# Feed-forward: the gated rows turned by VectorE in 32x32 blocks into SBUF, in place of fp32 transposes on TensorE through PSUM

## The reference

```python
h2 = _rmsnorm(x, g_ffn[l])
x = x + (jax.nn.silu(h2 @ w_ffn_gate[l]) * (h2 @ w_ffn_up[l])) @ w_ffn_down[l]   # D_FF = 2816
```

## Time and profile before

| | us |
|---|---|
| three runs | 1134.68, 1134.51, 1134.10 |
| median | 1134.51 |
| profiled execution | 1134.34 |
| its span | 1132.5 |
| TensorE busy | 1120.9 (99%) |
| VectorE busy | 710.5 (63%) |
| ScalarE busy | 633.9 (56%) |
| GpSimd busy | 213.2 (19%) |

### The profile page before, as it was taken

The page is one execution under the profiler, slowest core; times in us unless marked ns, Lnnn a source line. Parts: engine busy times, 40 slices in busy tenths (PEclk is TensorE's granted clock), DMA queues, the critical chain, the costliest instruction groups (busy, mean ns, idle before and its releaser), DMA issues.

```text
span 1132.5 us, 14165 instructions
## 1 busy us (share of the span) xinstructions
PE 1120.9 (99%) x5380; PEld 931.6 (82%) x5380; DVE 710.5 (63%) x721; ACT 633.9 (56%) x787; POOL 213.2 (19%) x127
## 2 busy tenths in 40 slices
PE   8999999999999999999999999999999999999998
PEld 7788887888888888888778888888888888888886
DVE  5745758676554543695338568984465776798442
ACT  6655566655767642654478365663355545566431
POOL 1424700000343410000013012420006100333000
PEclk9999999999999999999999999999999999999999
DMA  9644444545555455565434545565555334465630
GB/s 355 232 170 176 153 145 146 207 172 198 183 180 195 173 198 186 212 243 186 149 112 162 191 172 214 191 222 186 187 192 198 117 143 167 154 218 186 223 112 37
DMA packets 30502, 205.14 MB, mean 181 GB/s; under 512 B 3625, under 2 KB 3793, under 8 KB 6769
## 3 DMA queue, kind: packets, MB, share of 16 engines
q1 hardware_dynamic: 28752, 198.75, 48.8%
q0 software_dynamic: 1696, 5.64, 1.6%
HBM read 203.33 MB, written 1.05 MB: 180 GB/s over the span
## 4 chain that ended last, share of the span: by engine, by line
PE 93%; DVE 2%; issue 2%; POOL 1%; DMA 1%; ACT 1%; SPq 0%; DVEq 0%; POOLq 0%
PE ps L689 72%; PE ps L1185 8%; PE ps L1187 4%; PE aux L761 3%; PE ps L811 1%; PE aux L976 1%; PE aux L962 1%; DMA mrows<-in_mem 1%; DMA grow<-in_b_gate 1%; POOL sc L510 0%; PE aux L1123 0%; PE aux L1074 0%; DVE Wl L1867 0%; DVE sc L1939 0%; PE aux L1137 0%
## 5 line engine op out<-in xcount | busy, mean ns | idle before, releaser
L1867 DVE TENSOR_TENSOR Wl<-raw,Wh 128x2048 fp32r<-128x2048 f32 x184 | 451.9, 2462 | 255.4 <-ACT Wh L1318 254.9
L689 PE MATMUL ps<-Wh,xT 128*128 128x512 f32 x1536 | 486.7, 393 | 0.0
L1318 ACT ACTIVATE Wh<-raw 128x2048 fp32r<-128x2048 f32 x184 | 350.0, 1907 | 231.7 <-PE ps L689 228.5
L689 PEld LDWEIGHTS ps<-Wh,xT 128*128 128x128 f32 x1536 | 288.4, 188 | 60.3 <-issue 1.2
L689 PE MATMUL ps<-Wl,xT 128*128 128x512 f32 x768 | 299.0, 389 | 0.0
L689 PEld LDWEIGHTS ps<-Wl,xT 128*128 128x128 f32 x768 | 144.3, 188 | 29.4 <-issue 0.5
L1185 PE MATMUL ps<-xT,Wh 128*128 128x512 f32 x384 | 133.6, 394 | 0.0
L1187 PE MATMUL ps<-xT,Wl 128*128 128x256 f32 x384 | 106.4, 277 | 0.0
L689 PE MATMUL ps<-Wh,hTh 128*128 128x512 f32 x256 | 99.7, 389 | 0.0
L689 PE MATMUL ps<-Wh,hTl 128*128 128x512 f32 x256 | 99.6, 389 | 0.0
L689 PE MATMUL ps<-Wl,hTh 128*128 128x512 f32 x256 | 99.6, 389 | 0.0
(11 more groups left out here) (359 smaller groups left out, 1363.7 us busy)
## 6 DMA issues: line engine op xcount, KB each, us to landing
raw<-in_wstream SPq DMA_DIRECT2D x185, 1024.0 KB, 4.7
grow<-in_post_gains POOLq DMA_DIRECT2D x4, 512.0 KB, 5.8
grow<-in_b_gate POOLq DMA_DIRECT2D x6, 256.0 KB, 3.5
mrows<-in_mem SPq DMA_DIRECT2D x2, 512.0 KB, 5.4
raw<-in_wstream SPq DMA_DIRECT2D x2, 512.0 KB, 6.5
x<-in_x SPq DMA_DIRECT2D x1, 1024.0 KB, 13.4
out<-x SPq DMA_DIRECT2D x4, 256.0 KB, 2.0
rdm<-in_ret_decays POOLq DMA_DIRECT2D x1, 768.0 KB, 5.4
```

The source lines that it names most:

```text
L689: mm = nc.tensor.matmul(ps[2 * pair + t][:, :], a[:, kt, t * P:(t + 1) * P], w[:, slot, j, :], start=(first and j == 0 and q == 0), stop=( ...
L1318: nc.scalar.activation(Wh[:, slot, 0:nk, :], raw[:, slot, 0:nk, :], ACT.Copy).then_inc(hi_ready, 1)
L1867: nc.vector.tensor_tensor(Wl[:, slot, 0:nk, :], raw[:, slot, 0:nk, :], Wh[:, slot, 0:nk, :].bitcast(F32), ALU.subtract).then_inc(lo_ready, 1)
```

## The change

The gated rows don't go through TensorE and PSUM. VectorE turns them: 16 instructions, each of which takes a block of 32 partitions (tokens 32a to 32a+31 of both token tiles) and 32 columns of each of the two k-tiles, 128 elements per partition, turns it in 32x32 blocks and writes it to partitions 32b to 32b+31 of a new SBUF tile `ffT` with two buffers. They follow in `ff` behind the second low part of the granules and wait for `ff_h`. The log-sigmoid moves ahead of the first low part, `ff_low(n-1)` between the two. ScalarE's `ff_high` and VectorE's `ff_low` read `ffT` in place of `aux`; ScalarE's wait ahead of the read-outs is for the turn of unit n-2. TensorE has no transposes in this stage; before each granule of `ffd0` it waits for the low parts by a count.

```diff
--- before.py
+++ after.py
@@ -163,8 +163,6 @@
     use("foT", [0, 1, 2, 3])
     use("mgT", [0, 1, 2, 3])
     use("x1T", [0, 1, 2, 3])
-    for n in range(FFN // 256):
-        use(f"ffT{n}", [n % 2])
     use("x2T", [0, 1, 2, 3])
     use("rqT0", [0, 1])
     use("rqT1", [2, 3])
@@ -354,6 +352,7 @@
         ffTl = at("ffTl", [P, FFK, TOK], R + 22, F32R)
         gu = at("gu", [P, 2, 2, C], R + 44)
         fe = at("fe", [P, 2, 2, 256], R + 52)
+        ffT = at("ffT", [P, 2, 2, TOK], R + 56)
         RQ = at("RQ", [P, 2, D], R)
         RK = at("RK", [P, 2, D], R + 8)
@@ -1050,7 +1049,7 @@
                           (1, 0): half_ready("mgT", 2), (1, 1): half_ready("mgT", 3), (1, 2): next_tile("x1T", x, added("wout1"), 0)})
-            def ff_unit(n, i=None, between=None):
+            def ff_unit(n, i=None):
                 name = f"ffn{n}"
@@ -1060,35 +1059,18 @@
                 for q in range(2):
                     g = G[name] + q
-                    if q and between:
-                        between()
                     granule(g % RING, g + 1 if i is None else i * 4 + (g + 1), xTh, xTl, range(4 * q, 4 * q + 4),
                             U[name] % 2, q == 0, q == 1, read_out)
-            def ff_turned(n, i=None):
-                pe.wait_ge(sem("ff_h"), n + 1 if i is None else i * 2 + (n + 1))
-                k, use = AUX[(f"ffT{n}", 0)]
-                pe.wait_ge(aux_free[k], use - 1 if i is None else i + (use - 1))
-                for kk in range(2):
-                    for t in range(2):
-                        tr = nc.tensor.transpose(aux[k][:, kk * TOK + t * P:kk * TOK + (t + 1) * P],
-                                                 gu[:, n % 2, t, kk * P:(kk + 1) * P], ident)
-                tr.then_inc(aux_ready[k], 1)
             begin(["ffn0", "ffn1"], "x1T", x, added("wout1"))
-            ff_unit(2, None, lambda: ff_turned(0))
-            ff_turned(1)
+            ff_unit(2)
             with pe.Fori(1, 5) as i:
                 for n in (1, 2):
                     ff_unit(n, i)
-                    ff_turned(n - 1, i)
             def ff_ready(q):
                 def go_on():
-                    if q == 3:
-                        ff_turned(10)
-                    for n in range(2 * q, min(2 * q + 2, FFN // 256)):
-                        wait_operand(f"ffT{n}", (0,))
+                    pe.wait_ge(sem("ff_low"), min(2 * q + 2, FFN // 256))
                 return go_on
             product("ffd0", (ffTh, ffTl), before={q: ff_ready(q) for q in range(6)})
@@ -1587,7 +1569,7 @@
                 split(G[name] + RING, i)
                 count = n if i is None else i * 2 + n
                 if n >= 2 or i is not None:
-                    act.wait_ge(sem("ff_h"), count - 1)
+                    act.wait_ge(sem("ff_turned"), count - 1)
                 for t in range(2):
                     if t == 0:
                         act.wait_ge(half_done, count + (U["ffn0"] + 1))
@@ -1608,11 +1590,10 @@
                 nc.scalar.activation(fe[:, n % 2, :, :], fe[:, n % 2, :, :], ACT.Exp).then_inc(sem("ff_rec"), 1)
             def ff_high(n, i=None):
-                k, use = AUX[(f"ffT{n}", 0)]
-                act.wait_ge(aux_ready[k], use if i is None else i + use)
+                count = n if i is None else i * 2 + n
+                act.wait_ge(sem("ff_turned"), count + 1)
                 dst = ffTh[:, :, :].rearrange("p (n k) t -> p n k t", k=2)
-                nc.scalar.activation(dst[:, n if i is None else i * 2 + n, :, :], aux[k][:, :], ACT.Copy)\
-                    .then_inc(sem("ffT_hi"), 1)
+                nc.scalar.activation(dst[:, count, :, :], ffT[:, n % 2, :, :], ACT.Copy).then_inc(sem("ffT_hi"), 1)
             act.wait_ge(sem("norm_rstd"), NORMS["x1"])
             ff(0)
@@ -2196,31 +2177,41 @@
             cross(GEND["wout1"], "x1T", "g_ffn", mixed)
             x_stats("x1")
-            def ff(n, i=None):
+            def ff(n, i=None, low=True):
                 name = f"ffn{n}"
+                log_sigmoid(fe[:, n % 2, :, :], gu[:, n % 2, :, 0:256], n + 2 if i is None else i * 2 + (n + 2))
                 split(G[name] + RING, i)
-                log_sigmoid(fe[:, n % 2, :, :], gu[:, n % 2, :, 0:256], n + 2 if i is None else i * 2 + (n + 2))
+                if low:
+                    ff_low(n - 1, i)
                 split(GEND[name] - 1 + RING, i)
+                ff_turn(n, i)
+            def ff_turn(n, i=None):
+                dve.wait_ge(sem("ff_h"), n + 1 if i is None else i * 2 + (n + 1))
+                for a in range(4):
+                    for b in range(4):
+                        ins = nc.vector.transpose(ffT[32 * b:32 * b + 32, n % 2, :, :].rearrange("p k (t j) -> p k t j", j=P)
+                                                  [:, :, :, 32 * a:32 * a + 32],
+                                                  gu[32 * a:32 * a + 32, n % 2, :, 0:256].rearrange("p t (k j) -> p k t j", j=P)
+                                                  [:, :, :, 32 * b:32 * b + 32])
+                ins.then_inc(sem("ff_turned"), 1)
             def ff_low(n, i=None):
-                k, use = AUX[(f"ffT{n}", 0)]
                 count = n if i is None else i * 2 + n
                 dve.wait_ge(sem("ffT_hi"), count + 1)
                 lo = ffTl[:, :, :].rearrange("p (n k) t -> p n k t", k=2)
                 hi = f32(ffTh).rearrange("p (n k) t -> p n k t", k=2)
-                nc.vector.tensor_tensor(lo[:, count, :, :], per_kt(aux[k], 2), hi[:, count, :, :], ALU.subtract)\
-                    .then_inc(aux_free[k], 1)
-            ff(0)
+                nc.vector.tensor_tensor(lo[:, count, :, :], ffT[:, n % 2, :, :], hi[:, count, :, :], ALU.subtract)\
+                    .then_inc(sem("ff_low"), 1)
+            ff(0, low=False)
             ff(1)
-            ff_low(0)
             ff(2)
-            ff_low(1)
             with dve.Fori(1, 5) as i:
                 for n in (1, 2):
                     ff(n, i)
-                    ff_low(n - 1, i)
             for g in range(G["ffd0"], GEND["ffd0"] - 1):
                 split(g + RING)
                 if g == G["ffd0"] + 2:
```

## The result

| | us |
|---|---|
| before, median of 4 runs | 1134.47 (1134.1 to 1134.68) |
| after, median of 4 runs | 1150.27 (1149.67 to 1151.29) |
| ratio | 1.0142, 95% interval 1.0129 to 1.0154 |
| predicted | 1151 (1133 to 1168) |
| span of the profiled execution, before / after | 1132.5 / 1147.9 |

A forecast was written before the change was run, and what follows sets the result against it. TensorE (99% busy) bounds the kernel before; after the change VectorE sets the pace at 13.0 us a unit against 10.92. From 1134.34 us, -4.8 of transposes and +21.8 of stalls give +17, so 1151 us (1133 to 1168).

The forecast's parts named there:

- The removed term: TensorE's four transposes in each of 11 units, 0.44 us a unit, all on the path: 4.8 us saved.
- The price of a transpose: VectorE, 16 per unit: 0.32 us each from start to start, a turn of 5.1 us (3.4 to 6.6).
- The exclusion: VectorE and GpSimd instructions with two SBUF inputs exclude each other in the loop; 2.3 us of VectorE's period.
- My sequence of who waits for whom: Per unit: log-sigmoid, split to 2.90, first product 4.07, subtraction 4.63, second product 5.8, second split 7.96, transposes to 13.0 us.
- The period: VectorE's time per feed-forward unit: 13.0 us against TensorE's 10.92, so VectorE sets the pace.
- the sum: Whole feed-forward stretch: -4.8 us of transposes and +21.8 of stalls, +17 us, giving 1151 us.
- First stall: TensorE ahead of unit 3: split done at 308.1, TensorE free at 306.4, 1.7 us lost.
- the 21.8 I had as stalls: TensorE waiting for VectorE's splits, some 2 us in each of eleven places, +21.8 us.
- The first: Rival, VectorE: order blocks but transposes overlap at 0.21 us each, period 11.3, 1132 us; chance 0.11.
- The second: Rival: VectorE keeps up, no exclusion that matters, period 10.8, TensorE is the bound, 1129.6 us; chance 0.07.
- The third: Rival, VectorE: a transpose is dearer than the reduction, 0.36 to 0.45 us, 1158 to 1174 us; chance 0.15.
- The fourth: Rival: TensorE's granted clock falls because of the stalls, adding to the rest, over 1174 us; chance 0.04.

The follow-up runs named there:

- the first attempt: Kernel after, VectorE's queue reordered so the transposes of unit n-1 run beside GpSimd's products of n: 1133.44 us, ratio 0.9987.
- the run without the ring: Kernel after, transposes beside GpSimd's products, ScalarE's copy and VectorE's subtraction one unit later, down product's first split ahead of unit 10's transposes: 1129.72 us, ratio 0.9964.

## Why the prediction was right

**The removed term** was put at 4.8 us and is 4.8 us by the run with one transpose of four, taken from 33 transposes to all 44.

**The price of a transpose** was put at 0.32 us from start to start, out of a reduction's 286 ns and a gap of 0.03. Measured: 0.317, that is 302 ns and a gap of 0.015. The sum is right, the parts are not quite: the length is 16 ns more than the reduction's, the gap half of what I took. The reason given, that a change of partitions keeps neighbours from overlapping, is borne out by the run in which they stay: 0.195. The rule of the Trainium skill ("VectorE: DVE Perf Modes", Two Vector instructions with no wait between them) says this of the start of either input or output, and the runs agree: 0.317 us with either change, 0.195 us with neither. It says that such an instruction starts only when the earlier ones have finished, and the starts 14 ns behind the end, against 65 ns before it, agree as well; that the length also falls by 43 ns is something that the traces show and the rule doesn't name.

**The exclusion** was put at 2.3 us a period. Measured by taking the products away: 2.2 us. In the kernel after the subtraction carries 1.1 us of it and the second split the other 1.1. My sequence of who waits for whom is the one in the trace, within 0.1 us at each step. One forecast row is off: I expected both products to be recorded at over 2 us, and the second is 1.62 us, because it comes late in the subtraction and waits for only 0.3 us of it; the place that it ends at is as forecast. The page "SBUF — State Buffer" of the Trainium skill (SBUF: two separate sides) speaks of an exclusive lock that the one who starts first has for its whole instruction. The trace agrees: the subtraction isn't slowed, it ends 0.54 us after the product does.

**The period** was 13.0 us, measured 12.90; **the sum** +17 us, measured 15.3 us between the profiled executions and 16.1 us within the stretch. The 0.9 us between 17 and 16.1 are nine periods at 0.1 us too much. First stall: forecast 1.7 us, measured 1.53 (307.33 against 305.57 + 0.23). TensorE's idle time of 18.0 us is less than the 21.8 I had as stalls, but a stall costs more than its gap: the last matmul before it is recorded 0.39 us long where it holds the queue for 0.23, and the next matmul follows the first after it in 0.33 us in place of 0.23 (307.33 to 307.66). With an estimate of 0.25 us for each of 11 places it is 20.8 us, and 20.8 - 4.8 = 16.0.

**Rivals.** The first (transposes at 0.21 us, 1132 us) needed the partitions to stay; when they do for 12 of 16, the time is 1134.8. The second (VectorE keeps up, 1129.6 us) is what the kernel does once GpSimd's products are away: 1129.45. The third (a transpose dearer than the reduction, 0.36 us or more) falls with the 0.317 us measured. The fourth (the granted clock) didn't come, with stalls of up to 1.8 us each.

Left open: I haven't tried the kernel after with its subtraction reading PSUM, so what this operand by itself adds is not separated by a run. The first unit of the kernel after, which has no subtraction, allows an estimate:

```profile
291.83 0.69 DVE L1927 SCALAR_TENSOR_TENSOR fe<-gu,fe 128x512 f32<-128x512 f32 x1 [9.14 <-ACT fe L1587]
292.44 5.58 DVE L1848 TENSOR_TENSOR Wl<-raw,Wh 128x2048 fp32r<-128x2048 f32 x2
299.22 5.04 DVE L2195 STREAM_TRANSPOSE ffT<-gu 32x128 f32<-32x128 f32 x16 [1.19 <-POOL gu L595]
```

Its turn starts 7.39 us after the log-sigmoid, behind the wait for GpSimd's second product; in the loop it is 7.82 us. A subtraction that reads PSUM would run beside the first product and should leave the 7.39 as they are, so the operand costs an estimated 0.4 us a period, some 4 us in all, and not the 1.1 us for which it is blocked.

## What to carry to other kernels

Before work is moved to an engine that looks half idle, add up its period in the stage, start to start, and look for the same instruction at two lengths in its rows and in those of the engine beside it: here a product at 1.30 and 2.95 us told of 2.2 us a period that no busy share shows. Where the load then nearly fills the period, the order in the queue decides between a loss and a gain: the same 176 transposes make the kernel 15.8 us slower behind the splits, and 4.5 us faster beside GpSimd's products once ScalarE's copy and the last turn are placed to match. After such a reordering look at every engine that waits for the moved step, since the first attempt only moved the ring of waits to ScalarE.

## What the runs showed of the hardware

A VectorE transpose of 32 partitions x 128 fp32 elements takes 302 ns, and 260 ns when it begins on the partitions of the one before. Beginning elsewhere, at the input or the output, costs 0.12 us from start to start (0.317 against 0.195). It doesn't exclude GpSimd: two products of 1.30 and 1.29 us ran inside 16 transposes whose sum stayed at 5.04 us. Subtractions and splits with two SBUF inputs do: 1.78 us in place of 0.68, 3.38 in place of 2.28. A product of GpSimd that already waits goes first: the one recorded from 317.97 ends at 321.24, ahead of the subtraction issued at 320.00. The wait lies inside the recorded length, so it counts as busy time.

In the run with transposes beside the products, the stall of 2.2 us (from 415.7 to 417.8 us) was followed by TensorE at a lower granted clock. From the window table (us, busy of PE, PEld, DVE, ACT, POOL, clock):

```profile
400.00:420.00 20.00, 17.83 (x77) 14.23 (x76) 19.00 (x39) 11.69 (x12) 2.58 (x2) 0.98 0.45 163
420.00:440.00 20.00, 20.00 (x84) 16.36 (x83) 11.87 (x9) 6.82 (x4) 0.00 (x0) 0.93 0.86 317
```

The weight loads there are 0.33 us long from 419.67 to 422.23 us where they are 0.19 us before and behind, and 0.42 us apart where they are 0.23: TensorE at its lower level (1.2 GHz) for some 3 us, after 2.2 us without work. That is some 1.5 us on top of the stall. Stall and clock together (3.7 us in this execution) are more than the 2.6 us by which this run's ratio (0.9987) is above that of the run without the ring (0.9964); two of its eleven executions (1132.69 and 1132.19 us) had a granted clock of 1.000 over the span, so the clock's part isn't in all of them. The eleven shorter stalls of the kernel after left the clock at its upper level.
